# Sparse attention: scores from queries and keys split in two rounded parts, a head's high part and remainder stacked in 128 rows

## The chip, the cores and the metric

The kernel runs on one core of one Trainium2 chip. The metric is the device time of one execution in microseconds (us), as the median of several runs. All names of engines are those of the profile: PE is the matrix engine, PEld its weight loads, DVE the vector engine, ACT the scalar engine, POOL the GpSimd engine, SP the engine that queues the transfers.

## The reference, cut to what matters

The reference computes one block with pooling and sparse attention, and then a second block of two layers. Only the scores of the first block's attention are changed. Of its three branches (compressed, selected, window) the last two have, at 512 positions, scores of every query against every earlier key:

```
q  = partial_rope(rms_norm(q, q_norm_g), positions)      # 8 heads of 64, in 2 groups of 4
ks = partial_rope(rms_norm(k_sel, k_norm_g[1]), positions)   # one key head per group
kw = partial_rope(rms_norm(k_win, k_norm_g[2]), positions)
s = jnp.einsum('bqgrd,bgqkld->bgrqkl', qc, ksel) * scale     # selected blocks
p = masked_softmax(s, m_sel, (-2, -1))
s = jnp.einsum('bqgrd,bkgd->bgrqk', qc, kwc) * scale         # window
p = masked_softmax(s, m_win, -1)
return gc[..., 0:1] * o_cmp + gc[..., 1:2] * o_sel + gc[..., 2:3] * o_win
```

The sequence is 512 long, a head has 64 dimensions.

## The kernel before

**Numbers.** Activations lie transposed, channels on the 128 partitions and the 512 positions along the row. Every large product of weights and activations is made of three products in the rounded type F32R: both operands are split into a high part (rounded copy) and a remainder, and high by high, high by remainder and remainder by high are added in one accumulator bank. ACT makes the high part `wh` of a weight tile (`head`, line 1205) and POOL its remainder `wl` (`rest`, line 519, four instructions of 128x256 each). The scores are different: they are plain F32 products of the queries `qall` and the keys `kk`.

**Order of the first block.** PE works through tiles 0 to 11 of the input projection, then values and gates (`vg_highs`, `vg_lows`, tiles 12 to 14). Meanwhile DVE finishes norm and rotation of six pieces, in `rotated(0)` to `rotated(5)`: the two keys `kk[:, 0]` and `kk[:, 1]` and the four query pairs `qall[:, 0]` to `qall[:, 3]`. One such piece is 128x512: rows 0 to 63 belong to the head of group 0, rows 64 to 127 to that of group 1. Then comes the attention stage, 32 steps `p`, written out by hand: query pair j = p // 8, branch b = p // 4 % 2, query tile i = p % 4. Step p covers 128 queries against n = 128 (i + 1) keys.

**One step on PE** is: `score(p)`; in some steps `cmp_scores`, `values`, `cmp_turn`; `turn_probs(p - 2)`; and then `fill`, products of the pooling branch (lines 627, 628 and 633) that keep PE at work while DVE and ACT deal with the scores. `score(p)` makes one product for each group, the first from rows 0 to 63 and the second from rows 64 to 127, into the banks `SB[0]` and `SB[1]`, and first waits for the exponentials of step p - 1 (`exp_ready`), since there is one bank for each group.

**One step on the others.** DVE takes the masked maximum (`top`, line 1641), and normalizes the probabilities of the step before (`scale`, lines 1964 and 1967); in steps of j = 0 and 1 it also makes tables for the later layers (`steps(tables2, 2)`, lines 1696 to 1722). ACT makes the exponentials (`exps`, line 1361), and copies the turned probabilities (`puts`, line 1205). Every engine works through its list in order. All transfers are queued by SP; POOL issues none and does only `rest` here. The `sqacc` row is cleared by DVE early (line 1852) and used again after the attention.

Of the kernel before, what the change touches and what calls it, by code (L numbers as in the profile page):

```python
# [33 lines left out]
P = 128  # L34
# [124 lines left out]
def build(nc, x, positions, positions2, weights, par1, par2, consts, masks, masks2, w1, w2, pool_w, out):  # L159
    ctx = ExitStack()  # L160
    with ctx:
        base = -(-nc.sbuf_base // (4 * S)) * (4 * S)
        top = [base]

        def at(name, shape, dt, offset):
            return nc.alloc_sbuf_tensor_at(name, list(shape), dt, offset=offset)

        def sb(name, shape, dt=F32):
            size = int(np.prod(shape[1:])) * (2 if dt == BF16 else 4)
            t = at(name, shape, dt, top[0])  # L170
            top[0] += -(-size // 64) * 64
            return t

# [54 lines left out]
        def c2(name, i=0):  # L228
# [67 lines left out]
        hh = big("hh", 0, [P, KF, S], F32R)  # L296
        hl = big("hl", KF, [P, KF, S], F32R)

        cpad = big("cpad", 0, [P, 2, TAPS - 1 + S])
        conv = big("conv", 3, [P, 2, S])  # L300
        ya = big("ya", 5, [P, 2, S])
# [40 lines left out]
        x_landed = [sem(f"x_landed{i}") for i in range(4)]  # L342
        gains_landed = sem("gains_landed")
        par_landed = sem("par_landed")
        late_landed = sem("late_landed")
        cmsk_landed = sem("cmsk_landed")
        shift_landed = sem("shift_landed")
# [27 lines left out]
            "conv_ready", "silu_ready", "prod_ready", "h_hi", "h_lo",  # L375
            "glu_out", "tap_prod", "tap_added", "v_psum", "v_out", "v_rest", "rope_in", "lam_in", "lam_psum", "lam_exp", "lam_ready", "glu_sig", "conv_done", "conv_out",
            "qk_ready", "head_normed", "ya_ready", "ln_sub", "ln_sq", "ln_scaled", "yc_ready", "y_hi", "y_lo",
            "zeroed", "warm", "first_hi", "first_lo", "row_scale", "half_tile", "last_added", "last_sq", "last_sum", "pool_bc", "rstd_out", "pool_out", "out_ready", "par_ready")}
        R = ready
        block = ctx.enter_context(nc.Block())  # L380

# [129 lines left out]
        def _(pool):  # L511
# [24 lines left out]
                x_.then_inc(lo_ready, 1)  # L536

            first_rest()
            with pool.Fori(1, T_BLOCK1) as t:
                rest(Count(0).loop(t, 1))  # L540

            for l in range(LAYERS):
                T = Count(T_BLOCK1).loop(l, T_LAYER)
# [31 lines left out]
        def _(pe):  # L575
# [315 lines left out]
            def score(p):  # L891

                j, b, i = p // 8, p // 4 % 2, p % 4
                n = (i + 1) * P
                if p:
                    pe.wait_ge(R["exp_ready"], 2 * p)
                for g in range(2):
                    h = slice(g * 64, (g + 1) * 64)
                    mm(SB[g][:, 0:n], qall[h, j, i * P:n], kk[h, b, 0:n], start=True, stop=True)\  # L899
                        .then_inc(R["s_psum"], 1)  # L900

            def cmp_scores(j):
# [300 lines left out]
        def _(act):  # L1203
# [98 lines left out]
            def tile_root(m):  # L1302
                root(Count(m - 1), 8, scale=1.0 / 64)

            act.wait_ge(chunk_done, 4)
            head(Count(5))
            tile_square(2, 1)
# [12 lines left out]
            for n in range(6, N_IN):  # L1320
                act.wait_ge(chunk_done, n + 1)
                head(Count(n + 2))
                if n < 9:
                    tile_root(n - 1)
                if n < 8:
                    tile_square(n, n + 1)
                if n in (9, 10):
                    hidden_cmp(n - 9)
                if n == 11:
                    act.wait_ge(R["cmp_copied"], 1)  # L1330
                    act.activation(csq, kcf, ACT.Square).then_inc(sq_ready, 1)
                    act.wait_ge(R["vct_psum"], 1)
                    copy(vct, BC[0:64, 0:P]).then_inc(R["vct_ready"], 1)
                    root(Count(7), 2, parts=32, scale=1.0 / 64)
                if n == 13:
                    act.activation(small[:, 190:191], zero, ACT.Tanh)
                if 10 <= n < 14:
                    pool_head(n - 10)
                if n == 13:
                    act.wait_ge(R["row_scale"], 1)  # L1340
                    vg_out(0, vg_psum, 1, tile_out)
                    vg_out(3, vg_psum, 2, tile_out)
                    vg_out(2, vg_psum, 3, tile_out)
                    vg_out(1, chunk_done, T_IN, tr_read)
# [38 lines left out]
            for p in range(NP):  # L1383
                j, k = p // 8, p % 8
                t, n = T_IN + 3 * j, N_IN + 4 * j
                exps(p)
                if k == 1:
                    act.wait_ge(R["c_sub"], j + 1)
                    act.activation(cmp_p[:, :, :], cmp_p[:, :, :], ACT.Exp).then_inc(R["c_exp"], 1)
                if k == 4:  # L1390
                    act.wait_ge(R["c_tpsum"], j + 1)
                    copy(cmp_pt[:, :], TR[0:64, :]).then_inc(R["c_tready"], 1)
                if p >= 2:
                    puts(p - 2)
                if k == 0 and j:
                    next_head(t - 1)
                if k == 2 and j:
                    out_head(j - 1)
                if k in (3, 6):
                    next_head(t + k // 3 - 1)  # L1400
                if k in (4, 7):
                    gate(n, 0 if k == 4 else 1)
# [230 lines left out]
        def _(dve):  # L1633
# [129 lines left out]
            def rotated(i):  # L1763
                dve.wait_ge(turn1_landed[i % 2], 64 * (i // 2 + 1))
                tt(tmp2[:, 0:S], turned1[:, i % 2, :], sin[:, :], ALU.mult).then_inc(rot_read, 1)
                dve.drain()
                tt(dsts[i], tmp2[:, 0:S], cosp[:, i % 2, :], ALU.add)

            dsts = [kk[:, 0, :], kk[:, 1, :]] + [qall[:, c, :] for c in range(4)]
            gains = [c1("sel_g"), c1("win_g")] + [q_g8] * 4  # L1770
# [78 lines left out]
            dve.drain()  # L1849
            for m in (2, 3, 0, 1):  # L1850
                take(Count(3), Count(m), kvraw[:, m, :] if m < 2 else ybuf[:, m % 2, :], bank_=X4[m])
            dve.memset(sqacc[:, :], 0.0)
            steps(tables1, 2)
            pair_recips(Count(1), 8)
            steps(tables1, 1)
# [119 lines left out]
            for p in range(NP):  # L1975
# [17 lines left out]
                if j < 2 and k not in (0, 2):  # L1993
                    if p == 1:
                        dve.wait_ge(late_landed, 16 * 7)
                    steps(tables2, 2)
            scale(NP - 1)
            pool_gated(NT - 1, 1)
            out_rest(NT - 1)
# [471 lines left out]
```

## Time and profile before

| what | value |
|---|---|
| median of 3 runs | 1873.36 us (1872.85 to 1874.01) |
| the profiled execution | 1872.83 us, span 1871.0 us |
| PE, PEld | 1854.5 us (99%), 1500.5 us (80%) |
| POOL | 1106.2 us (59%) |
| DVE | 856.4 us (46%) |
| ACT | 728.6 us (39%) |
| attention stage, first score to last | 109.1 to 245.3 us |

Busy time of PE is the union of its instructions' times, and its matmuls are pipelined, so 99% doesn't mean that each product runs at its best rate. The time from one instruction's start to the next one's start, which the timeline shows, says what an instruction costs PE.
### The profile page before, as it was taken

To read this page: it belongs to the slowest core of one execution; us is meant where nothing else is said; L and a number is where in the kernel's file an instruction comes from. 1 tells how busy PE (TensorE), PEld (TensorE's weight loads), DVE (VectorE), ACT (ScalarE), POOL (GpSimd) and SP (SyncE) were. 2 spreads that over 40 slices of the span, in tenths; PEclk is the share of its full clock that TensorE was granted. 3 is DMA by queue.
4 is the path that set the end of the run, shared out by engine and by line. 5 is a ranking of instruction groups with operands and counts; after the bars stand their busy time and mean duration, and the time that the engine had idled before them with its cause. 6 is when DMAs were issued, how large, how long until landed. Compare 5 with 4: busy or idle time off the path is not lost.

```text
span 1871.0 us, 28766 instructions
## 1 busy us (share of the span) xinstructions
PE 1854.5 (99%) x8696; PEld 1500.5 (80%) x8696; DVE 856.4 (46%) x1383; ACT 728.6 (39%) x1169; POOL 1106.2 (59%) x1312
## 2 busy tenths in 40 slices
PE   9999999999999999999999999999999999999998
PEld 8866678888888888767888888888867888888887
DVE  7887644465555122876532333112776533333112
ACT  5255543433232223475432323232476433232222
POOL 5532245566667565875656565666775565655654
PEclk9999999999999999999999999999999999999999
DMA  7221123322332333321223322333422223222332
GB/s 268 65 70 46 45 71 99 101 91 91 99 97 93 113 101 102 113 80 57 90 91 100 101 90 101 101 102 102 122 66 71 90 90 101 90 101 92 103 109 79
DMA packets 52407, 177.50 MB, mean 95 GB/s; under 512 B 6832, under 2 KB 8112, under 8 KB 52080
## 3 DMA queue, kind: packets, MB, share of 16 engines
q1 hardware_dynamic: 52336, 176.57, 28.9%
q8 instruction: 43, 0.70, 0.2%
q14 instruction: 28, 0.23, 0.0%
HBM read 168.84 MB, written 2.10 MB: 91 GB/s over the span
## 4 chain that ended last, share of the span: by engine, by line
PE 92%; DVE 4%; ACT 2%; DVEq 1%; issue 1%; DMA 0%; POOL 0%; SPq 0%; POOLq 0%; ACTq 0%
PE bank L613 23%; PE bank L593 23%; PE bank L594 23%; PE bank L650 3%; PE bank L657 3%; PE bank L651 3%; PE bank L899 1%; PE bank L946 1%; PE bank L627 1%; PE bank L628 1%; PE bank L932 1%; PE bank L633 1%; PE bank L734 1%; PE bank L721 1%; PE bank L713 1%; PE bank L714 1%
## 5 line engine op out<-in xcount | busy, mean ns | idle before, releaser
L519 POOL TENSOR_TENSOR wl<-raw,wh (+1 forms) x1240 | 1014.6, 849 | 717.6 <-ACT wh L1205 717.1
L1205 ACT ACTIVATE wh<-raw 128x1024 fp32r (+2 forms) x312 | 329.9, 1058 | 823.1 <-PE bank L613 678.0
L593 PE MATMUL bank<-xh,wh 128*128 128x512 f32 x1312 | 514.0, 392 | 0.0
L594 PE MATMUL bank<-xl,wh 128*128 128x512 f32 x1312 | 510.9, 389 | 0.0
L613 PE MATMUL bank<-xh,wl 128*128 128x512 f32 x1312 | 332.2, 392 | 0.0
L593 PEld LDWEIGHTS bank<-xh,wh 128*128 128x128 f32 x1312 | 246.8, 188 | 52.1 <-ACT lv L1205 0.7
L594 PEld LDWEIGHTS bank<-xl,wh 128*128 128x128 f32 x1312 | 246.4, 188 | 50.5
L613 PEld LDWEIGHTS bank<-xh,wl 128*128 128x128 f32 x1312 | 243.9, 188 | 51.7 <-issue 2.5
L593 PE MATMUL bank<-hh,wh 128*128 128x512 f32 x506 | 196.8, 389 | 0.0
L594 PE MATMUL bank<-hl,wh 128*128 128x512 f32 x506 | 196.8, 389 | 0.0
L1685 DVE TENSOR_TENSOR ybuf<-bank,rstd 128x512 f32<-128x512 f32 x92 | 63.3, 689 | 226.1 <-PE bank L613 223.8
L2022 DVE TENSOR_TENSOR xs<-xs,bank 128x512 f32<-128x512 f32 (+1 forms) x47 | 31.4, 684 | 235.9 <-PE bank L613 188.3
L613 PE MATMUL bank<-hh,wl 128*128 128x512 f32 x506 | 125.9, 389 | 0.0
L613 PEld LDWEIGHTS bank<-hh,wl 128*128 128x128 f32 x506 | 95.0, 188 | 19.7
L594 PEld LDWEIGHTS bank<-hl,wh 128*128 128x128 f32 x506 | 95.0, 188 | 19.7
L593 PEld LDWEIGHTS bank<-hh,wh 128*128 128x128 f32 x506 | 95.0, 188 | 19.7
L2062 DVE TENSOR_TENSOR tmp<-tmp,ybuf 128x512 f32<-128x512 f32 x66 | 71.7, 1086 | 73.3 <-ACT tmp L1460 73.0
L553 POOL TENSOR_TENSOR conv<-conv,tprod 128x512 f32<-128x512 f32 x60 | 83.7, 1395 | 26.0 <-ACT tprod L1205 18.2
L2064 DVE TENSOR_TENSOR hl<-tmp,hh 128x512 f32 (+1 forms) x66 | 60.8, 922 | 58.7 <-ACT hh L1205 58.7
L1685 DVE TENSOR_TENSOR tmp<-bank,rstd 128x512 f32<-128x512 f32 x78 | 53.8, 690 | 59.6 <-PE bank L613 40.6
L1205 ACT ACTIVATE hh<-tmp 128x512 f32 (+1 forms) x66 | 41.8, 633 | 82.0 <-DVE tmp L2062 82.0
L650 PE MATMUL bank<-xh,wh 128*128 128x512 f32 x160 | 62.8, 393 | 0.0
(337 smaller groups left out, 2334.3 us busy)
## 6 DMA issues: line engine op xcount, KB each, us to landing
raw<-in_weights SPq DMA_DIRECT2D x311, 512.0 KB, 3.4
turned<-ybuf SPq DMA_DIRECT2D x64, 64.0 KB, 2.0
xs<-in_x SPq DMA_DIRECT2D x4, 512.0 KB, 6.7
out_t<-outs SPq DMA_DIRECT2D x8, 256.0 KB, 2.3
w1k<-in_w SPq DMA_DIRECT2D x1, 1024.0 KB, 9.5
w1v<-in_w SPq DMA_DIRECT2D x1, 1024.0 KB, 11.0
shifted<-kvraw SPq DMA_DIRECT2D x8, 124.0 KB, 2.3
posi<-in_positions SPq DMA_DIRECT2D x2, 256.0 KB, 8.7
```

Source lines behind the costliest of these rows:

```text
L519: x_ = pool.tensor_tensor(wl[:, :, :].rearrange("p s n -> p (s n)")[:, two], raw[:, cols((v % 4) * (CB * P) + h * part, part)], wh[:, :, : ...
L553: pool.tensor_tensor(conv[:, 1, :], conv[:, 1, :], tprod[:, k % 4, :], ALU.add)\
L593: mm(b[:, :], w, kh(k), start=first and k == 0, stop=False)
L594: mm(b[:, :], w, kl(k), start=False, stop=False)
L613: i = mm(b[:, :], wl[:, s, (blk0 + k) * P:(blk0 + k + 1) * P], kh(k), start=False, stop=last and k == blocks - 1)
L650: mm(X4[a][:, :], w, kh(k), start=k == 0, stop=False)
L651: mm(X4[a][:, :], w, kl(k), start=False, stop=False)
L657: i = mm(X4[a][:, :], wl[:, s, (4 * kk + a) * P:(4 * kk + a + 1) * P], kh(2 * c + kk), start=False, stop=c == 3 and kk == 1)
L1205: return act.activation(o, i, ACT.Copy, scale=scale)
L1685: return tt(o, b[:, :], rstd[:, :], ALU.mult).then_inc(tile_out, 1)
L2062: tt(tmp[:, 1, :], tmp[:, 0, :], ybuf[:, 0, :], ALU.mult).then_inc(R["prod_ready"], 1)
L2064: tt(flat(hl)[:, cols(j * S, S)], tmp[:, 1, :], flat(hh)[:, cols(j * S, S)].bitcast(F32), ALU.subtract).then_inc(R["h_lo"], 1)
```

## The change

Each of the six pieces gets a stacked form and a low part, both in F32R. For query pair or key i, `STACKED[i][g]` is 128x512: for a query, the rows of the group's own half hold its high part and the other 64 rows hold its remainder; for a key, both halves hold the high part. `LOW_PART[i]` is the remainder. A score is then, for each group, one product over 128 rows (high and remainder of the query by the high part of the key) and one over 64 rows (high part of the query by the remainder of the key), added in the same bank.

ACT copies the high parts (`high_part`), POOL subtracts (`low_part`) and moves 64 rows of each to the other half with two transfers from its own queue, six pieces in all. DVE only signals. The clearing of `sqacc` moves to the end of the attention, since its place holds a stacked key.

```diff
+        STACKED = [[row(f"stacked{i}{g}", place) for g, place in enumerate(pair)] for i, pair in enumerate((
+            (45, where["sqacc"]), (39, 43), (46, where["cos"]), (38, 41), (12, 13), (39, 43)))]
+        LOW_PART = [row(f"low_part{i}", place) for i, place in enumerate((8, 42, 9) + 3 * (where["sin"],))]
+        PART_OF = [kk[:, 0, :], qall[:, 0, :], kk[:, 1, :], qall[:, 1, :], qall[:, 2, :], qall[:, 3, :]]
+        KEY_PART, QUERY_PART = (0, 2), (1, 3, 4, 5)
...
             first_rest()
-            with pool.Fori(1, T_BLOCK1) as t:
-                rest(Count(0).loop(t, 1))
+            def low_part(i):
+
+                pool.wait_ge(R["part_hi"], i + 1)
+                if i > 3:
+                    pool.wait_ge(part_landed[i - 1], 32)
+                pool.tensor_tensor(LOW_PART[i], PART_OF[i], STACKED[i][0].bitcast(F32), ALU.subtract)\
+                    .then_inc(R["part_lo"], 1)
+                pool.wait_ge(R["part_lo"], i + 1)
+                for half, dest in enumerate(STACKED[i]):
+                    own, other = slice(half * 64, half * 64 + 64), slice(64 - half * 64, 128 - half * 64)
+                    moved = dest if i in KEY_PART else LOW_PART[i]
+                    pool.dma_start(dest[other, :], moved[own, :]).then_inc(part_landed[i], 16)
+
+            at_ = 1
+            for end, parts in ((12, (0,)), (13, (1,)), (17, (2, 3)), (20, (4,)), (23, (5,)), (T_BLOCK1, ())):
+                with pool.Fori(at_, end) as t:
+                    rest(Count(0).loop(t, 1))
+                for i in parts:
+                    low_part(i)
+                at_ = end
...
                 if p:
                     pe.wait_ge(R["exp_ready"], 2 * p)
+                key, query = KEY_PART[b], QUERY_PART[j]
+                if p in (0, 4):
+                    pe.wait_ge(part_landed[key], 32)
+                if i == 0 and b == 0:
+                    pe.wait_ge(part_landed[query], 32)
+                for g in range(2):
+                    mm(SB[g][:, 0:n], STACKED[query][g][:, i * P:n], STACKED[key][g][:, 0:n], start=True, stop=False)
                 for g in range(2):
                     h = slice(g * 64, (g + 1) * 64)
-                    mm(SB[g][:, 0:n], qall[h, j, i * P:n], kk[h, b, 0:n], start=True, stop=True)\
+                    mm(SB[g][:, 0:n], STACKED[query][g][h, i * P:n], LOW_PART[key][h, 0:n], start=False, stop=True)\
                         .then_inc(R["s_psum"], 1)
...
+            def high_part(i):
+
+                act.wait_ge(R["kq_ready"], (1, 3, 2, 4, 5, 6)[i])
+                a, b = STACKED[i]
+                copy(a, PART_OF[i])
+                copy(b[64:128, :], PART_OF[i][64:128, :]).then_inc(R["part_hi"], 1)
+
...
                 if n in (9, 10):
                     hidden_cmp(n - 9)
+                    high_part(n - 9)
...
                 if p >= 2:
                     puts(p - 2)
+                if p == 1:
+                    act.wait_ge(rot_read, 7)
+                    high_part(2)
+                if p == 2:
+                    high_part(3)
+                if p == 10:
+                    act.wait_ge(R["part_lo"], 4)
+                    high_part(4)
+                if p == 18:
+                    high_part(5)
...
-                tt(dsts[i], tmp2[:, 0:S], cosp[:, i % 2, :], ALU.add)
+                tt(dsts[i], tmp2[:, 0:S], cosp[:, i % 2, :], ALU.add).then_inc(R["kq_ready"], 1)
...
-            dve.memset(sqacc[:, :], 0.0)
             steps(tables1, 2)
...
                     steps(tables2, 2)
+            dve.memset(sqacc[:, :], 0.0)
             scale(NP - 1)
```

The pieces are numbered in the order of `PART_OF`: 0 and 2 are the keys, 1, 3, 4 and 5 the query pairs.

## Rows read from the trace of the kernel before

**Rows 1.** The page: span, and busy time of each engine.
```profile
span 1871.0 us, 28766 instructions
...
PE 1854.5 (99%) x8696; PEld 1500.5 (80%) x8696; DVE 856.4 (46%) x1383; ACT 728.6 (39%) x1169; POOL 1106.2 (59%) x1312
```

**Rows 2.** Busy time by stretch: length, PE, PEld, DVE, ACT, POOL, granted clock, DMA.
```profile
178.00:214.00 36.00, 36.00 (x201) 23.84 (x200) 23.45 (x81) 19.96 (x58) 8.46 (x13) 1.00 0.13 45
```

**Rows 3.** Timeline of PE, the three scores that it waits for.
```profile
124.00 0.49 PE L899 MATMUL bank<-kk,qall 64*128 64x128 f32 x4 [0.18 <-ACT probs L1361]
...
131.72 0.92 PE L899 MATMUL bank<-kk,qall 64*128 64x384 f32 x4 [0.64 <-ACT probs L1361]
...
163.91 0.70 PE L899 MATMUL bank<-kk,qall 64*128 64x256 f32 x4 [0.41 <-ACT probs L1361]
```

**Rows 4.** Timeline of PE, 180 to 211 us.
```profile
180.34 0.40 PE L628 MATMUL bank<-xl,wh 128*128 128x512 f32 x1
...
183.07 0.39 PE L628 MATMUL bank<-xl,wh 128*128 128x512 f32 x1
183.38 0.70 PE L899 MATMUL bank<-kk,qall 64*128 64x256 f32 x4
184.02 1.09 PE L932 MATMUL bank<-cst,probs 128*128 128x128 f32 x8
...
196.19 0.49 PE L899 MATMUL bank<-kk,qall 64*128 64x128 f32 x4
196.61 0.88 PE L932 MATMUL bank<-cst,probs 128*128 128x128 f32 x6
197.25 0.48 PE L627 MATMUL bank<-xh,wh 128*128 128x512 f32 x1
...
205.90 1.12 PE L951 MATMUL bank<-cmp_pt,small 64*128 64x512 f32 x2
...
209.15 1.13 PE L899 MATMUL bank<-kk,qall 64*128 64x512 f32 x4
210.21 0.66 PE L932 MATMUL bank<-cst,probs 128*128 128x128 f32 x4
```

**Rows 5.** Timeline of PE in the last tile, F32R products of 256 columns.
```profile
1849.04 2.08 PE L1048 MATMUL bank<-hh,wl 128*128 128x256 f32 x16
1850.96 0.28 PE L1042 MATMUL bank<-hh,wh 128*128 128x256 f32 x1
```

**Rows 6.** Timeline of ACT, 115 to 123 us.
```profile
115.95 0.42 ACT L1389 ACTIVATE cmp_p<-cmp_p 128x256 f32<-128x256 f32 x1 [0.56 <-DVE cmp_p L1928]
118.51 0.58 ACT L1361 ACTIVATE probs<-bank,small 128x384 f32<-128x384 f32 x1 [2.14 <-DVE small L1641]
...
122.49 0.69 ACT L1361 ACTIVATE probs<-bank,small 128x512 f32<-128x512 f32 x1 [2.41 <-DVE small L1641]
```

**Rows 7.** Timeline of POOL around the stage's first steps.
```profile
111.74 2.80 POOL L519 TENSOR_TENSOR wl<-raw,wh  x4 [2.38 <-ACT wh L1205]
125.80 3.83 POOL L519 TENSOR_TENSOR wl<-raw,wh  x4 [11.26 <-ACT wh L1205]
```

**Rows 8.** The page: costliest groups, and transfers.
```profile
L553 POOL TENSOR_TENSOR conv<-conv,tprod 128x512 f32<-128x512 f32 x60 | 83.7, 1395 | 26.0 <-ACT tprod L1205 18.2
...
L1205 ACT ACTIVATE hh<-tmp 128x512 f32 (+1 forms) x66 | 41.8, 633 | 82.0 <-DVE tmp L2062 82.0
...
shifted<-kvraw SPq DMA_DIRECT2D x8, 124.0 KB, 2.3
```

**Rows 9.** Timeline of DVE, beside POOL at work until 213.1 us and behind it.
```profile
212.41 0.95 DVE L1967 TENSOR_SCALAR probs<-probs,small,small 128x512 f32<-128x512 f32 x1
...
213.51 0.55 DVE L1967 TENSOR_SCALAR probs<-probs,small,small 128x512 f32<-128x512 f32 x1
```

**Rows 10.** Timelines of DVE and of PE at the start.
```profile
35.11 0.48 DVE L1852 MEMSET sqacc<- 128x512 f32 x1
...
37.95 0.66 PE L742 MATMUL bank<-cst,pairs 128*128 128x128 f32 x4 [0.32 <-DVE pairs L1669]
```

More of the change, by code:

```diff
@@ L163, in build @@
         top = [base]
+        where = {}
         def at(name, shape, dt, offset):
@@ L170, in sb @@
             t = at(name, shape, dt, top[0])
+            where[name] = top[0]
             top[0] += -(-size // 64) * 64
@@ L297, in build, with row @@
         hl = big("hl", KF, [P, KF, S], F32R)
+        PART_OF = [kk[:, 0, :], qall[:, 0, :], kk[:, 1, :], qall[:, 1, :], qall[:, 2, :], qall[:, 3, :]]
+        def row(name, place):
+            return at(name, [P, S], F32R, place if place > 100 else BIG + place * UNIT)[:, :]
+        STACKED = [[row(f"stacked{i}{g}", place) for g, place in enumerate(pair)] for i, pair in enumerate((
+            (45, where["sqacc"]), (39, 43), (46, where["cos"]), (38, 41), (12, 13), (39, 43)))]
+        LOW_PART = [row(f"low_part{i}", place) for i, place in enumerate((8, 42, 9) + 3 * (where["sin"],))]
+        KEY_PART, QUERY_PART = (0, 2), (1, 3, 4, 5)
         cpad = big("cpad", 0, [P, 2, TAPS - 1 + S])
@@ L344, in build @@
         par_landed = sem("par_landed")
+        part_landed = [sem(f"part_landed{i}") for i in range(6)]
         late_landed = sem("late_landed")
@@ L377, in build @@
             "qk_ready", "head_normed", "ya_ready", "ln_sub", "ln_sq", "ln_scaled", "yc_ready", "y_hi", "y_lo",
-            "zeroed", "warm", "first_hi", "first_lo", "row_scale", "half_tile", "last_added", "last_sq", "last_sum", "pool_bc", "rstd_out", "pool_out", "out_ready", "par_ready")}
+            "zeroed", "kq_ready", "part_hi", "part_lo", "warm", "first_hi", "first_lo", "row_scale", "half_tile", "last_added", "last_sq", "last_sum", "pool_bc", "rstd_out", "pool_out", "out_ready", "par_ready")}
         R = ready
```

## The prediction

> **What bounds the kernel now.** I read the page first: PE is busy 1854.5 of 1871.0 us [rows 1], so time is gained only where PE is kept shorter, or made to wait less. Then the busy times by stretch: from 178 to 214 us, in the middle of the attention stage, PE is busy 36.00 of 36 us, while no other engine reaches 24 [rows 2]. There a microsecond less on PE is a microsecond less in the end. Before that it is not so: PE waits for exponentials in steps 4, 6 and 13, together 1.23 us [rows 3], because DVE makes tables there beside its share of the scores. Last, the timeline of PE, start to start, gives what the score products cost.
>
> **What the scores cost now.** From the start of a score to the start of what follows it, 128, 256 and 512 columns take 0.42, 0.64 and 1.06 us [rows 4]. This is 0.207 us plus 1.667 ns a column; that slope is four passes at 2.4 GHz (0.417 ns a column each). 384 columns are then 0.85. A score comes 0.31 us after a product that costs 0.2275 (twelve of them in 2.73 us, 180.34 to 183.07), so entering it costs 0.085 more [rows 4]. The two groups run side by side: one 64-row product of 512 columns alone (line 951) lasts 1.12 us, and the two of a score 1.13 [rows 4]. So the four lengths, entry included, are 0.505, 0.725, 0.932 and 1.145 us, 3.31 in all, eight times over.
>
> **What they cost after.** F32R makes one pass instead of four, but there are two products now, and the 128-row ones of the two groups fill the array and go one after the other.
> - Two 128-row products: 2 x 0.2275 at 512 columns [rows 4], 2 x 0.120 at 256 (sixteen in 1.92 us) [rows 5], the middle, 2 x 0.174, at 384. No row has F32R at 128 columns. The nearest are the transposes of 128 columns, six in 0.64 us, 0.107 each [rows 4]; twice the 256 is the other end in time per column, four passes a third (0.213). I take 0.107: the array is no emptier than there, and the weights are of the same size.
> - Entering the 64-row products: 0.085, as now. The 128-row ones follow the fill products in the same form, so they pay no entry.
> - The 64-row pair, side by side: one pass, 0.053, 0.107, 0.160, 0.213. That F32R pairs also overlap is in no row; if not, it costs a full product more (0.107 to 0.2275), 0.63 for four lengths.
> - The constant 0.207: an F32 product is two records, an F32R one only one. I take it as 0.104 for each round of records, so half of it goes. The ends are none of it gone and all of it gone, 3.3 us up or down in 32 steps.
>
> Sums: 0.46, 0.54, 0.70 and 0.86, together 2.55 instead of 3.31. Eight times 0.76 is **6.1 us less on PE**.
>
> **What of it is lost.** Savings of steps 2 to 6 (0.24 + 0.29 + 0.05 + 0.19 + 0.24 = 1.0) come before waits that DVE and ACT set [rows 3]; PE just waits longer. For step 13 I count 0.2 more. 1.2 us are lost; nothing to 2 are the bounds.
>
> **Piece by piece.** Each piece is two copies on ACT, 0.63 us each by the nearest form [rows 8], some 1.2 us. Pieces 0 and 1 are made while the projection runs; they are wanted only at 109 us. Piece 2 comes at step 1, behind the exponential that starts at 115.95 and lasts 0.42, so it ends at 117.6; the next exponential isn't due before 118.51, for ACT waits 2.14 us there. Piece 3 comes at step 2, behind two small copies, at 120.0, and ends at 121.3, before 122.49 [rows 6]. Pieces 4 and 5 stand in the same sort of gap; behind piece 4 stands `out_head(0)`, which is wanted a step later. ACT costs nothing; without these gaps it would be up to 1.2 us a piece.
>
> POOL subtracts: 1.4 us a piece [rows 8]. Beside it DVE slows: the same operation takes 0.95 us with POOL at work and 0.55 without [rows 9]. This counts only where DVE sets the time, pieces 2 and 3; one operation on the path each, 2 x 0.4 = **0.8 us more** (0 to 1.6). The work itself fits: POOL is free from 114.5 to 125.8 [rows 7]. The wait for `part_hi` holds back `rest(12)`, `rest(13)`, `rest(17)`, `rest(20)` and `rest(23)`, and so the remainders that PE wants and the weight loads behind them on SP; each has some microseconds until it is due, since PE first does the tile's high products.
>
> Twelve transfers of 128 KB are issued by POOL. No row has a transfer from POOL; SP's 124 KB one lands 2.3 us after its issue [rows 8]. Piece 2 is the only tight one: subtracted at 117.6 + 1.4 = 119.0, landed at 121.3 by that row, wanted by step 4 at 124.00 [rows 3]. That leaves 2.7 us for what POOL needs to issue two transfers. I cost it at nothing; once the cover is gone, each microsecond later is one at the end. The Trainium skill, page "SBUF — State Buffer", section "SBUF: two separate sides", has a rule against this: GpSimd writes its own descriptors, and while VectorE runs an operation that takes the shared port it can't. No row shows it, for POOL issues nothing before the change. By it the landing moves by the operations met, 0.55 us each [rows 9]: four of them are 2.2 us and still inside the 2.7, so the sum stays, and of the late landing's chance below half is owed to it.
>
> The cleared `sqacc` leaves the start: 0.48 us of DVE [rows 10] ahead of a PE wait of 0.32 us; **0.3 us less** (nothing to 0.3). At its new place DVE waits for the last exponential anyway.
>
> **The sum.** -6.1 + 1.2 + 0.8 - 0.3 = **-4.4 us**. The profiled execution took 1872.83 us (span 1871.0 and 1.83 around it), 0.5 below the median of 1873.36. From that median: **1869.0 us**, 0.23% less. What a measurement of this kernel can tell from no change is about 0.2%, 3.75 us; the forecast is just past it.
>
> **Rivals.**
> - *Narrow products cost more.* If F32R at 128 columns makes four passes, the two 128-row products cost 2 x 0.106 more and the pair 0.160: 0.37 in eight steps, 3.0 us. For it: no row under 256 columns. Against: 0.120 at 256 shows no step upwards. 1872.0 us.
> - *The constant stays.* The entry and exit of a 64-row group, not the records, make up the 0.207: 3.3 us more, 1872.3.
> - *The 64-row pair doesn't overlap in F32R.* 8 x 0.63 = 5.0 more: 1874.0. Against: F32 does overlap in the same rows and banks.
> - *Slower: piece 2 lands late.* POOL takes long to issue, and step 4 stands still. Place: the wait for `part_landed[2]`. It eats the gain of 4.4 when it lands at 128.4 + the 2.7 of cover counted, that is 7.1 us behind my estimate of 121.3, and is slower by over 0.2% from 10.9 behind on; at 13 us the end is 1879. For it: nothing bounds POOL's issue from above. Against: SP's transfer of the same size took 2.3 us in all [rows 8], a fifth of what it needs.
> - *Larger gain.* All of the constant goes: 1865.7.
>
> **How the numbers follow.** Forecast 0.58, on its own between 1867 and 1870.5, two thirds of it past the bound; narrow products 0.12; constant stays 0.12; no overlap 0.07; late landing 0.06 (0.04 of it slower), larger gain 0.05. The predicted time is 1869.0. Down to 1866.3 and up to 1873.8 leaves out half of the larger gain, the late landing and most of no overlap, under 0.2. Faster by over 0.2%: 0.58 x 0.66 + 0.05 = 0.43. Slower: 0.05. The same: 0.52.
>
> **What the profile after would show.** Score groups of 0.46, 0.54, 0.70 and 0.86 us, start of the first 128-row product to the next instruction; the 64-row pair with starts a few nanoseconds apart; waits for ACT before steps 4, 6 and 13 grown to some 2.4 us; no wait of PE for a transfer; the wait at 37.95 gone. I am wrong if the 128-column products take over 0.15 us each, if the 64-row products come one after the other, or if PE stands still for `part_landed`.

## The result, and the profile after

The changed kernel takes 1876.54 us (median of 22 runs, 1874.19 to 1877.89); the kernel before takes 1873.24 beside it (22 runs, 1872.35 to 1874.10). The ratio is 1.0018, with a 95% interval of 1.0013 to 1.0024: 3.3 us slower, where 4.4 us less was forecast. The result lies outside the range, and its sign is the other one. One of the eleven runs of "piece 1 later" below took 3226.41 us at a mean granted clock of 0.647, and its ratio leaves that run out.

The profiled execution took 1876.28 us. Its page answers to [rows 1] as follows; the last line is the new queue of POOL.

```profile
span 1874.4 us, 28801 instructions
...
PE 1854.7 (99%) x8696; PEld 1510.0 (81%) x8696; DVE 860.3 (46%) x1383; ACT 735.4 (39%) x1181; POOL 1120.6 (60%) x1330
...
q0 software_dynamic: 960, 1.57, 0.4%
```

The span is 3.4 us longer and PE is busy for as long as before, so on the page alone nothing seems to have become faster. The waits of PE over the first 262 us say more (total, times, longest):

```profile
PE bank L869 <- DVE ybuf L1741: 3.4, 1, 3.4
PE bank L934 <- ACT probs L1407: 3.3, 4, 1.4
```

The first is new. The second answers to [rows 3], which had 1.23 us in three. The timeline of PE shows where they lie, and where the attention stage begins and ends:

```profile
37.23 0.60 PE L773 MATMUL bank<-cst,pairs 128*128 128x128 f32 x4
...
98.20 0.40 PE L869 MATMUL bank<-wh,xh 128*128 128x280 f32 x1 [3.36 <-DVE ybuf L1741]
...
103.42 0.29 PE L869 MATMUL bank<-wh,xh 128*128 128x280 f32 x1
...
113.47 0.33 PE L934 MATMUL bank<-stacked,stacked 128*128 128x128 f32 x2
...
125.26 0.73 PE L934 MATMUL bank<-stacked,stacked 128*128 128x512 f32 x2 [1.35 <-ACT probs L1407]
...
130.48 0.44 PE L934 MATMUL bank<-stacked,stacked 128*128 128x128 f32 x2 [1.19 <-ACT probs L1407]
...
144.43 0.61 PE L934 MATMUL bank<-stacked,stacked 128*128 128x512 f32 x2
...
248.41 0.63 PE L934 MATMUL bank<-stacked,stacked 128*128 128x512 f32 x2
```

In the kernel before, the scores of steps 0, 7 and 31 (the last two have 512 columns) start at 109.13, 138.28 and 244.22 us. These three starts cut the execution into four stretches, and each stretch answers one question:

| stretch | before | after | difference |
|---|---|---|---|
| start to step 0: projection, with pieces 0 and 1 | 109.13 | 113.47 | +4.34 |
| step 0 to 7: DVE and ACT set the time, pieces 2 and 3 | 29.15 | 30.96 | +1.81 |
| step 7 to 31: PE sets the time | 105.94 | 103.98 | -1.96 |
| step 31 to the end of the span | 1626.8 | 1626.0 | -0.8 |

**The gain is there, in the third stretch, but small.** Three lengths of score groups in that stretch, start of the first 128-row product, start of the 64-row pair, start of what follows:

```profile
148.18 0.33 PE L934 MATMUL bank<-stacked,stacked 128*128 128x128 f32 x2
148.45 0.33 PE L937 MATMUL bank<-low_part,stacked 64*128 64x128 f32 x2
148.71 0.28 PE L948 MATMUL bank<-cmsk 128*128 128x256 bf16 x1
...
153.54 0.40 PE L934 MATMUL bank<-stacked,stacked 128*128 128x256 f32 x2
153.87 0.39 PE L937 MATMUL bank<-low_part,stacked 64*128 64x256 f32 x2
154.18 1.09 PE L970 MATMUL bank<-cst,probs 128*128 128x128 f32 x8
...
162.21 0.63 PE L934 MATMUL bank<-stacked,stacked 128*128 128x512 f32 x2
162.77 0.50 PE L937 MATMUL bank<-low_part,stacked 64*128 64x512 f32 x2
163.20 0.66 PE L970 MATMUL bank<-cst,probs 128*128 128x128 f32 x4
```

The groups take 0.53, 0.64 and 0.99 us, and the one of 384 columns 0.81 (156.96 to 157.77): 2.97 for the four lengths, where 2.55 was forecast and 3.31 were needed before. At 512 columns the two 128-row products take 0.56, of which 2 x 0.2275 = 0.455 is the products; the pair takes 0.43, of which 0.213 is one pass over 512 columns. So about 0.1 is lost on the way into the pair and 0.2 on the way out.

**The first loss: one small DVE operation.** DVE in the first stretch, and then POOL (there, and beside steps 1 and 2 of the attention):

```profile
91.85 1.63 DVE L1839 TENSOR_TENSOR tmp<-tmp 128x512 f32<-128x512 f32 x1
...
94.17 2.94 DVE L1845 TENSOR_TENSOR small<-tmp,cst 128x16 f32<-128x16 f32 x1
...
97.45 0.69 DVE L1741 TENSOR_TENSOR ybuf<-bank,rstd 128x512 f32<-128x512 f32 x1
```

```profile
91.19 1.74 POOL L557 TENSOR_TENSOR low_part<-qall,stacked 128x512 fp32r<-128x512 f32 x1
93.23 1.06 POOL L563 DMA_DIRECT2D stacked<-low_part  x2 [0.29 <-POOL low_part L557]
94.30 2.77 POOL L532 TENSOR_TENSOR wl<-raw,wh  x4
...
121.97 1.29 POOL L557 TENSOR_TENSOR low_part<-kk,stacked 128x512 fp32r<-128x512 f32 x1 [2.98 <-ACT stacked L1243]
123.56 1.06 POOL L563 DMA_DIRECT2D stacked<-stacked  x2 [0.30 <-POOL low_part L557]
126.79 1.28 POOL L557 TENSOR_TENSOR low_part<-qall,stacked 128x512 fp32r<-128x512 f32 x1 [2.17 <-ACT stacked L1243]
```

The 128x16 operation of line 1845 takes 0.17 us elsewhere (at 85.67). Here it takes 2.94 and ends at 97.11, when the four back-to-back instructions of `rest(13)` end on POOL (94.30 + 2.77 = 97.07). Behind it on DVE stands the operation that empties PE's bank (97.45), and PE waits 3.36 us for that. In the kernel before DVE was 0.99 us ahead of POOL here; DVE's operation and `rest(13)`:

```profile
93.81 0.17 DVE L1789 TENSOR_TENSOR small<-tmp,cst 128x16 f32<-128x16 f32 x1
```

```profile
94.80 3.96 POOL L519 TENSOR_TENSOR wl<-raw,wh  x4 [2.23 <-ACT wh L1205]
```

Now DVE is 0.4 us later, held at 91.85 beside the subtraction of piece 1 (1.63 us), and `rest(13)` is 0.5 us earlier, so that they start 0.13 us apart, DVE first.

**The pause costs more than its length.** Busy times by stretch just behind it (length, PE, PEld, DVE, ACT, POOL, granted clock, DMA):

```profile
98.80:100.00 1.20, 1.20 (x5) 0.81 (x4) 1.05 (x3) 0.00 (x0) 0.00 (x0) 0.51 0.88 348
100.00:102.00 2.00, 2.00 (x7) 0.87 (x6) 1.74 (x5) 0.23 (x1) 0.00 (x0) 0.50 0.04 12
102.00:103.00 1.00, 1.00 (x8) 1.00 (x8) 0.52 (x1) 0.98 (x2) 0.00 (x0) 0.88 0.00 0
```

The granted clock is 0.50, the level of 1.2 GHz, from 98.8 to some 102.2 us; in the kernel before it is 1.00 in this stretch. From the product that waited (98.20) to the first product of the next tile (103.42) PE takes 5.22 us; the same instructions took 3.56 before (95.41 to 98.97). These are 1.66 us more. So the first stretch is 3.36 + 1.66 - 0.7 (from the earlier start at 37.23) = 4.3 longer.

**The second loss: steps 2 and 3.** The two halves of DVE's `scale`, one not beside a subtraction and one beside it, in step 2 and in step 3:

```profile
121.32 0.41 DVE L2022 TENSOR_SCALAR probs<-probs,small,small 128x256 f32<-128x256 f32 x1
...
121.88 1.53 DVE L2022 TENSOR_SCALAR probs<-probs,small,small 128x256 f32<-128x256 f32 x1
...
126.15 0.48 DVE L2022 TENSOR_SCALAR probs<-probs,small,small 128x384 f32<-128x384 f32 x1
...
126.78 1.50 DVE L2022 TENSOR_SCALAR probs<-probs,small,small 128x384 f32<-128x384 f32 x1
```

They take 1.1 and 1.0 us longer and end 0.15 and 0.2 us behind the end of POOL's subtraction (121.97 + 1.29 = 123.26, and 128.07). [Rows 9] had shown 0.4 for such a meeting.

**What held.** ACT's copies lie in the gaps: the exponential behind the first pair of copies waits 2.08 us for DVE, not for ACT.

```profile
120.63 1.26 ACT L1243 ACTIVATE stacked<-kk 128x512 fp32r<-128x512 f32 x2
123.98 0.58 ACT L1407 ACTIVATE probs<-bank,small 128x384 f32<-128x384 f32 x1 [2.08 <-DVE small L1697]
```

POOL issues two transfers in 1.06 us (1.22 for the pair of piece 0), and they land 2.4 us after issue (last number):

```profile
stacked<-low_part POOLq DMA_DIRECT2D x8, 128.0 KB, 2.4
...
stacked<-stacked POOLq DMA_DIRECT2D x4, 128.0 KB, 2.4
```

Piece 2 is thus there about 127.0 us (issue from 123.56, 1.06, 2.4), and step 4 wants it at 130.48. PE has no wait for a transfer.

**The last stretch differs, though its code is the same.** In the second block PE has pauses that differ between the profiled executions. From 745 to 860 us, before and then after:

```profile
745.00:860.00 115.00, 112.89 (x549) 85.03 (x548) 90.99 (x151) 76.02 (x153) 89.07 (x91) 1.00 0.29 89
```

```profile
745.00:860.00 115.00, 114.56 (x556) 87.40 (x555) 87.48 (x147) 73.55 (x149) 91.69 (x95) 1.00 0.30 92
```

PE is idle 2.1 us in the one and 0.4 in the other, but the changed kernel does the same work 4.2 us later, and a pause of 0.5 us that lies inside the window before lies behind it after. Over the whole last stretch PE is idle 11.5 us before and 10.8 after, which is the difference of 0.8. Between 1624.9 and 1627.7 us lie the last stretches of all the kernels below. A single span therefore doesn't settle a difference of less than some 3 us; the first three stretches are compared for that, beside the medians.

### The profile page after: what moved, and what is told of

It reads as the page before. It is cut to its first block, busy times and chain, and to the rows that moved or that the text cites. A ratio compares the mean times of both kernels' runs of the same rounds, so it can differ in the third digit from the quotient of the medians.

```text
span 1874.4 us, 28801 instructions
## 1 busy us (share of the span) xinstructions
PE 1854.7 (99%) x8696; PEld 1510.0 (81%) x8696; DVE 860.3 (46%) x1383; ACT 735.4 (39%) x1181; POOL 1120.6 (60%) x1330
## 4 chain that ended last, share of the span: by engine, by line
PE 91%; DVE 5%; ACT 2%; DVEq 1%; issue 1%; DMA 0%; SPq 0%; POOL 0%; POOLq 0%; ACTq 0%
PE bank L644 23%; PE bank L624 23%; PE bank L625 23%; PE bank L681 3%; PE bank L688 3%; PE bank L682 3%; PE bank L984 1%; PE bank L970 1%; DVE bank L1693 1%; PE bank L664 1%; PE bank L658 1%; PE bank L659 1%; PE bank L765 1%; PE bank L1160 1%; ACT lp L1587 1%
```

## The experiments

My theory after the result had three parts: **(A)** the products save 2.8 us in 32 steps, not 6.1, because the constant of 0.2 us stays whole, beside a way in of about 0.1; **(B)** the pause at 98.20 comes from the meeting of DVE with `rest(13)` that piece 1 brings about; **(C)** the subtractions of pieces 2 and 3 hold DVE in steps 2 and 3. The rivals: the products gave what was forecast and the rest is all contention, or the new waits are owed to something else (the transfers, the moved clearing, ACT's copies). Each ran against the kernel before on the same chip.

| kernel | ratio (95%) | median, before beside it | to step 0 | 0 to 7 | 7 to 31 | rest |
|---|---|---|---|---|---|---|
| before | | | 109.1 | 29.15 | 105.94 | 1626.8 |
| after | 1.0018 (1.0013 to 1.0024) | 1876.54, 1873.24 | 113.5 | 30.96 | 103.98 | 1626.0 |
| products alone | 0.9989 (0.9980 to 0.9998) | 1871.27, 1873.36 | 108.9 | 29.09 | 104.00 | 1627.5 |
| all but the products | 1.0030 (1.0018 to 1.0041) | 1878.39, 1873.36 | 112.2 | 31.03 | 105.94 | 1625.5 |
| piece 1 later | 1.0000 (0.9991 to 1.0010) | 1873.50, 1873.36 | 108.8 | 31.22 | 104.02 | 1627.1 |
| narrow subtraction | 0.9977 (0.9968 to 0.9986) | 1868.90, 1873.36 | 109.0 | 28.86 | 103.95 | 1625.1 |
| clearing alone | 0.9999 (0.9990 to 1.0008) | 1873.14, 1873.33 | 108.5 | 29.16 | 105.96 | 1627.7 |
| tables later | 0.9993 (0.9984 to 1.0002) | 1871.89, 1873.33 | 109.4 | 27.46 | 106.20 | 1627.6 |
| piece 1 and tables later | 0.9986 (0.9977 to 0.9995) | 1870.51, 1873.33 | 108.7 | 28.32 | 104.23 | 1627.6 |
| the same, DVE subtracts 2 and 3 | 0.9984 (0.9975 to 0.9993) | 1870.30, 1873.33 | 108.8 | 27.87 | 104.27 | 1627.6 |
| after, whole rows | 1.0002 (0.9993 to 1.0011) | 1873.62, 1873.33 | 114.6 | 30.88 | 101.26 | 1624.9 |
| DVE subtracts, whole rows | 0.9969 (0.9957 to 0.9981) | 1867.44, 1873.33 | 109.1 | 27.28 | 102.19 | 1626.6 |
| the same, group after group | 0.9966 (0.9954 to 0.9978) | 1866.80, 1873.33 | 108.7 | 27.12 | 101.48 | 1627.3 |

The four columns on the right are of the profiled executions, from the starts of the scores of steps 0, 7 and 31.

**The products alone.** The kernel before, with queries and keys written in F32R and the score as one 128-row and one 64-row product on them; no split, no copy, no transfer. The scores are those of rounded operands, and each has a product over 128 rows that mixes both groups.

```diff
+                    mm(SB[g][:, 0:n], qr[:, j, i * P:n], kr[:, b, 0:n], start=True, stop=False)
+                for g in range(2):
                     h = slice(g * 64, (g + 1) * 64)
-                    mm(SB[g][:, 0:n], qall[h, j, i * P:n], kk[h, b, 0:n], start=True, stop=True)\
+                    mm(SB[g][:, 0:n], qr[h, j, i * P:n], kr[h, b, 0:n], start=False, stop=True)\
```

> The kernel before with the new products alone: for each group a 128-row and a 64-row F32R product on the unstacked queries and keys. It leaves out splitting and stacking, so the sums in the banks are others; ACT, POOL and the transfers are as before. Theory A (the products gain about half of what was forecast, and POOL's work costs more than that): groups of 0.53, 0.64, 0.81 and 0.99 us instead of 0.505, 0.725, 0.93 and 1.145, 2.8 us less on PE, 0.7 of it swallowed by waits of the first steps: 2.1 us less, 0.9989 of before. Theory B (the products gain nothing in the end): 1.000. The forecast as made: 4.9 us less, 0.9974.

1871.27 us, 2.1 us less, ratio 0.9989. Steps 7 to 31 take 104.00 us, as in the changed kernel. (A) holds: the products give about 2 us, and 6.1 was never to be had from them.

**All but the products.** The changed kernel, with its pieces, copies and transfers, but with scores as F32 products of 64 rows on the high parts alone.

```diff
-                for g in range(2):
-                    mm(SB[g][:, 0:n], STACKED[query][g][:, i * P:n], STACKED[key][g][:, 0:n], start=True, stop=False)
...
-                    mm(SB[g][:, 0:n], STACKED[query][g][h, i * P:n], LOW_PART[key][h, 0:n], start=False, stop=True)\
+                    mm(SB[g][:, 0:n], STACKED[query][g][h, i * P:n].bitcast(F32), STACKED[key][g][h, 0:n].bitcast(F32), start=True, stop=True)\
```

> The changed kernel with plain F32 64-row products as before, on the stacked high parts; the remainders are made and moved, but left out of the scores. It holds all the overheads and none of the products' gain. Theory A: 2 us slower than the changed kernel, ratio to before 1.0028. Theory B (products worth nothing, overheads small): as the changed kernel, 1.0018.

1878.39 us, 5 us more than before: this is what making the pieces costs. Steps 7 to 31 are back at 105.94, to the hundredth; the pause of 3.4 us is there, and steps 0 to 7 are as long as in the changed kernel. Its profiled execution (1876.60 us) is the fastest of its seven, and its clock did not fall behind the pause (below). The two halves of the change add up: -2.1 and +5.0 make +2.9, and +3.3 was measured.

**Piece 1 later.** POOL subtracts piece 1 behind `rest(13)` instead of ahead of it.

```diff
-            for end, parts in ((12, (0,)), (13, (1,)), (17, (2, 3)), (20, (4,)), (23, (5,)), (T_BLOCK1, ())):
+            for end, parts in ((12, (0,)), (14, (1,)), (17, (2, 3)), (20, (4,)), (23, (5,)), (T_BLOCK1, ())):
```

> The changed kernel with piece 1 made by POOL behind the remainder of tile 13 instead of ahead of it. Theory A (POOL, late by piece 1, starts tile 13's four subtractions just as a short DVE operation is to begin, holds it for 2.8 us, and PE waits 3.4 us for the tile DVE takes next): the wait of 3.4 us goes, 2.5 to 3.4 us faster than the changed kernel, 1.0000 to 1.0005 of before. Theory C (the wait comes from ACT's copies or the transfers of piece 1): no change, 1.0018.

1873.50 us, 3.0 less than the changed kernel. The pause is gone, the granted clock is 1.00 from 94 to 104 us, and step 0 starts at 108.81 instead of 113.47. The operation that was held takes its usual time; the second line is the one that empties the bank:

```profile
93.47 0.17 DVE L1845 TENSOR_TENSOR small<-tmp,cst 128x16 f32<-128x16 f32 x1
...
93.98 0.69 DVE L1741 TENSOR_TENSOR ybuf<-bank,rstd 128x512 f32<-128x512 f32 x1
```

(B) is shown, as far as the order on POOL is its cause. Nothing was done to the length of `rest(13)` itself, and the hold also starts while POOL still issues the second transfer (until 94.29), which this edit moves as well; the next run bears on that.

**A narrow subtraction.** POOL subtracts 16 of 512 columns; the high part stands in the place of the remainder in the transfers and the products. The remainders are left out of the scores.

```diff
-                pool.tensor_tensor(LOW_PART[i], PART_OF[i], STACKED[i][0].bitcast(F32), ALU.subtract)\
+                pool.tensor_tensor(LOW_PART[i][:, 0:16], PART_OF[i][:, 0:16], STACKED[i][0][:, 0:16].bitcast(F32), ALU.subtract)\
...
-                    moved = dest if i in KEY_PART else LOW_PART[i]
+                    moved = dest
...
-                    mm(SB[g][:, 0:n], STACKED[query][g][h, i * P:n], LOW_PART[key][h, 0:n], start=False, stop=True)\
+                    mm(SB[g][:, 0:n], STACKED[query][g][h, i * P:n], STACKED[key][g][h, 0:n], start=False, stop=True)\
```

> The changed kernel with POOL's subtraction cut from 512 to 16 columns; the low part is left out of the scores (a high part stands in its place), copies, waits, transfers and products are all there. Theory A (the length of the subtraction holds DVE off its operations): the two DVE operations of 1.5 us in steps 2 and 3 are 0.4 to 0.5 again, and the wait of 3.4 us at 98 us goes or shrinks: 2 to 5.5 us faster than the changed kernel, 0.9989 to 1.0007 of before. Theory C (transfers or ACT's copies cost it): as the changed kernel, 1.0018.

1868.90 us. Both losses are gone: no pause at 98 us, though piece 1 and its transfers still stand ahead of `rest(13)` (DVE's small operation starts at 93.80, `rest(13)` at 94.75), and steps 0 to 7 take 28.86 us instead of 31.22 with piece 1 later. The operation beside POOL's subtraction in step 2, and that subtraction:

```profile
117.39 0.45 DVE L2022 TENSOR_SCALAR probs<-probs,small,small 128x256 f32<-128x256 f32 x1
```

```profile
117.46 0.22 POOL L557 TENSOR_TENSOR low_part<-kk,stacked 128x16 fp32r<-128x16 f32 x1 [2.98 <-ACT stacked L1243]
```

(C) is shown: 2.4 us in steps 0 to 7 hang on the length of the subtractions, and not on the copies or the transfers, which are all still there. The kernel was some 2 us faster than I had expected. In the profiled execution that lies in the last stretch, 1625.1 us against 1627.1, where its instructions are those of the others. The median shows the same 2 us, so it belongs to this kernel and not to one execution; its cause is open.

**The clearing alone.** The kernel before, with the clearing of `sqacc` moved.

```diff
-            dve.memset(sqacc[:, :], 0.0)
             steps(tables1, 2)
...
+            dve.memset(sqacc[:, :], 0.0)
             scale(NP - 1)
```

> The kernel before with the clearing of sqacc moved to the end of the attention, as in the change, and nothing else. As forecast: the PE wait of 0.3 to 0.6 us at 38 us goes, 0.9998. If it is worth 2 us, which the difference of the two earlier runs (new products alone, narrow subtraction) would allow, 0.9989.

1873.14 beside 1873.33 us, and the interval includes no change. In the profile the wait of 0.32 us [rows 10] is gone, and step 0 starts 0.6 earlier. It is no cause of a loss.

**Tables later.** The kernel before, with DVE's tables out of steps 0 to 7 and one instruction at a time in the steps behind.

```diff
-                if j < 2 and k not in (0, 2):
-                    if p == 1:
-                        dve.wait_ge(late_landed, 16 * 7)
-                    steps(tables2, 2)
+                if p == 1:
+                    dve.wait_ge(late_landed, 16 * 7)
+                if j and k not in (0, 2):
+                    steps(tables2, 1)
```

> The kernel before with DVE's table steps for the later layers taken out of the steps of query pair 0 and spread over those of pairs 1 to 3, one a step. Theory D (DVE's tables make PE wait in steps 4, 6 and 13): those waits of 1.2 us go, 0.9993. If another engine sets them: 1.000.

1871.89 us, 1.4 less; steps 0 to 7 take 27.46 instead of 29.15. So the waits of [rows 3] were DVE's own load, worth 1.4 us already in the kernel before.

**Both, in the changed kernel.** Piece 1 later and tables later.

> The changed kernel with piece 1 behind tile 13 and with the tables moved as in the run before. Theory A with D: DVE has 8 us less to do in pair 0, so POOL's two subtractions of 1.1 us each on its way are covered, and PE's waits of 3.6 us for exponentials shrink below 1.5 us: 2 to 3 us faster than with piece 1 alone moved, 0.9985 to 0.999 of before. If the waits come from the chain score, maximum, exponential itself: 1.000, as without the tables.

1870.51 us: 6.0 less than the changed kernel, 2.8 less than the kernel before. **The same, with pieces 2 and 3 subtracted by DVE** instead of POOL; in its profile each subtraction takes DVE 0.69 us.

```diff
+                if p in (2, 3):
+                    dve.wait_ge(R["part_lo"], p)
+                    dve.wait_ge(R["part_hi"], p + 1)
+                    tt(LOW_PART[p], PART_OF[p], STACKED[p][0].bitcast(F32), ALU.subtract).then_inc(R["part_lo"], 1)
```

> As the run before, but pieces 2 and 3 are subtracted by DVE itself behind its maxima of steps 2 and 3 (0.7 to 1.0 us each) and POOL only moves them. Theory A: no operation of DVE is held for over a microsecond in these steps, PE's waits go below 1 us: as the run before or up to 1 us faster, 0.998 to 0.9988 of before. A rival: piece 2 then lands some 2 us later than with POOL, and PE waits for it in step 4 by up to 1 us: 0.999.

1870.30 us. Steps 0 to 7 are 0.45 us shorter; in the medians the two can't be told apart.

**What is the constant?** A step of the prediction was still open: 0.207 us of each score, beside the 0.1 on the way in, that no count of columns explains. Either it is the way into and out of 64-row products, or it comes with each round of products on a bank. This tells them apart: the second product over all 128 rows, the stacked query by the whole row of the key's remainders. The added rows multiply the remainder of one group's query by the remainder of the other group's key, a term of second order.

```diff
-                    h = slice(g * 64, (g + 1) * 64)
-                    mm(SB[g][:, 0:n], STACKED[query][g][h, i * P:n], LOW_PART[key][h, 0:n], start=False, stop=True)\
+                    mm(SB[g][:, 0:n], STACKED[query][g][:, i * P:n], LOW_PART[key][:, 0:n], start=False, stop=True)\
```

> The changed kernel, with the second product of each group over all 128 rows instead of 64: stacked query by the whole row of key remainders. The rows that are added multiply a remainder of one group's query by a remainder of the other group's key. Theory (the 0.2 us constant of a score, and the 0.1 before it, are the way into and out of a 64-row product): no product of a score has 64 rows any more, both are gone, and a score is four products of 0.107, 0.120, 0.174 or 0.2275 us: groups of 0.43, 0.48, 0.70 and 0.91 us instead of 0.53, 0.64, 0.81 and 0.99, which is 0.45 x 8 = 3.6 us less, some 3 of it outside waits; ratio to before 1.0002 instead of 1.0018. Rival (the constant comes with each round of a score, whatever its rows): two more full products stand in place of a side-by-side pair, 0.16 + 0.13 + 0.19 + 0.24 = 0.72 a quartet, 5.8 us more; ratio 1.005.

1873.62 us, 2.9 less than the changed kernel, although PE now streams twice as many columns for the second product. Two groups of its timeline:

```profile
149.13 0.33 PE L934 MATMUL bank<-stacked,stacked 128*128 128x128 f32 x2
149.30 0.39 PE L936 MATMUL bank<-low_part,stacked 128*128 128x128 f32 x2
149.53 0.28 PE L947 MATMUL bank<-cmsk 128*128 128x256 bf16 x1
...
162.79 0.63 PE L934 MATMUL bank<-stacked,stacked 128*128 128x512 f32 x2
163.25 0.62 PE L936 MATMUL bank<-low_part,stacked 128*128 128x512 f32 x2
163.71 0.60 PE L969 MATMUL bank<-cst,probs 128*128 128x128 f32 x4
```

The groups take 0.40 and 0.92 us instead of 0.53 and 0.99, which is four products and hardly a constant; that of 256 columns takes 0.47 instead of 0.64. The one of 384 takes 0.79 instead of 0.81: behind it come products with a tile of 64 columns (128*64), and my reading is that the array's shape still changes there. No run was made for it, but in step 2 of this trace, where a 128*128 product follows (at 122.34), the group of 384 takes 0.71 us. Steps 7 to 31 take 101.26 us. The rival, 5.8 us more, is out. The Trainium skill, page "TensorEngine Tiling (Array Packing)", section "Key Properties", says that changing the tiling mode drains the engine; the trace agrees, and puts 0.1 us on the way in and 0.2 on the way out.

This run still has the pause at 98 us. Its clock there, and that of the run with everything but the products:

```profile
98.00:103.00 5.00, 4.58 (x15) 3.06 (x16) 4.19 (x12) 0.50 (x2) 0.00 (x0) 0.50 0.35 107
```

```profile
98.00:103.00 5.00, 4.63 (x31) 3.86 (x32) 4.38 (x14) 2.28 (x4) 0.00 (x0) 1.00 0.32 107
```

The first ran at half the clock throughout, the second at the full one, after the same pause. The pause thus costs 3.4 us plus something that is 0.1 us in one execution (98.37 to 102.05 for what took 3.56 before), 1.66 in another and 2.5 in a third (98.42 to 104.51). The 22 runs of the changed kernel spread over 3.7 us and those of before over 1.75, which fits.

**Whole rows in the best version so far** (piece 1 and tables later, DVE subtracts 2 and 3):

> The version with piece 1 behind tile 13, the tables spread over the later steps and pieces 2 and 3 subtracted by DVE (ratio 0.9984), with the second product of each group over all 128 rows. Theory: 3 us less than that version, ratio 0.9968. Rival (constant stays): 5.8 us more, ratio 1.0015.

1867.44 us, 2.9 less again.

**And the products of group 0 ahead of those of group 1:**

```diff
                 for g in range(2):
                     mm(SB[g][:, 0:n], STACKED[query][g][:, i * P:n], STACKED[key][g][:, 0:n], start=True, stop=False)
-                for g in range(2):
                     mm(SB[g][:, 0:n], STACKED[query][g][:, i * P:n], LOW_PART[key][:, 0:n], start=False, stop=True)\
                         .then_inc(R["s_psum"], 1)
```

> As the run before it, and the two products of group 0 ahead of the two of group 1, so that group 0's maximum can begin before group 1's products. Group 0's bank is complete 0.1 to 0.45 us earlier, group 1's at the same time. Theory: it counts only where PE waits for the exponentials, three or four steps: 0 to 0.5 us less than the run before it, ratio 0.9966. Rival (two products into one bank one behind the other cost more than two into different banks): 0.05 us or more for each of 32 steps, 1.6 us more, ratio 0.9977.

1866.80 us, the fastest: 6.4 to 6.5 less than the kernel before. Steps 7 to 31 are 0.7 us shorter than in the run before it. Two products into one bank one behind the other cost nothing extra: the groups keep their lengths, and the difference is shorter waits for ACT (0.4 instead of 1.1 us from 134 to 240).

## Why the prediction was wrong, step by step

- **"The constant 0.207 ... half of it goes": wrong, and 3.3 of the 6.1 us with it.** I took the constant for the count of records and named its other reading as a rival. It is the change of shape, and it stays whole: 2.97 us for four lengths where 3.31 were needed before and 2.55 forecast, so 0.34 x 8 = 2.7 us less instead of 6.1. The rival "the constant stays" was right on this term, with its 3.3 us. [Rows 4] had a hint that I read but did not use: behind a 128-row product a 64-row one started 0.085 us late, so a change of shape had a price on the way in, and might have had one on the way out.
- **"Pieces 0 and 1 ... are wanted only at 109 us": true, and the wrong question.** What mattered was what POOL's new work does to DVE at that time, 91 to 97 us. I had costed contention only "where DVE sets the time, pieces 2 and 3". DVE empties the banks of the projection as well, so it can set the time there too: 3.36 us of pause and 1.66 of lower clock. This is the largest term, and I had it at nothing. The work itself moved little: `rest(13)` merely came to stand a tenth of a microsecond behind a short operation of DVE that the bank was waiting for.
- **"2 x 0.4 = 0.8 us" for pieces 2 and 3: the mechanism was right, the size off.** The two operations took 1.1 and 1.0 us longer, 2.1 in all, and steps 0 to 7 were 2.4 us shorter in the run with the narrow subtraction. The 0.4 of [rows 9] was a meeting with the tail of POOL's instruction; a whole meeting lasts as long as the subtraction, 1.29 us. Both figures lie past my upper bound of 1.6.
- **What is lost in the first steps: right in kind.** With the products alone steps 0 to 7 take 29.09 us instead of 29.15, though their groups should be 0.6 us shorter by the rows above (0, 0.085, 0.125, 0.155 a length). But the waits before scores grow only from 1.23 to 1.45 us, in steps 3, 4, 6 and 13; the rest goes into groups behind a wait, which are 0.1 us longer, and into gaps behind the groups. In the changed kernel these waits are 3.3 us, where "some 2.4 us" was forecast: that the number comes near is chance, for most of it is the hold by the subtractions and not the swallowed gain.
- **The covers: right.** ACT costs nothing, and pieces 4 and 5 neither (105.94 us for steps 7 to 31 with everything but the products, as before); piece 2 has 3.5 us to spare, with POOL's issue taking 1.06 us for two transfers; no wait for `part_landed`. The sentence that the prediction takes from the Trainium skill, page "SBUF — State Buffer", section "SBUF: two separate sides", that VectorE can keep GpSimd from writing its descriptors, is not borne out here. The pairs of pieces 2 and 3 had no DVE operation of the kind that was held beside them, but where DVE subtracts, POOL issues the pair of piece 3 in 1.02 us from 123.97 on, beside such an operation, and neither is slower for it:

```profile
124.18 0.55 DVE L2023 TENSOR_SCALAR probs<-probs,small,small 128x512 f32<-128x512 f32 x1
```

- **The clearing: right**, 0.3 us in the wait, not to be told apart in the median.
- **F32R at 128 columns and the overlap of the 64-row pair: right.** Two products of 128 columns take 0.17 us where nothing changes shape (149.13 to 149.30), and the pair takes 0.26, 0.31 and 0.43 us at 128, 256 and 512 columns with its exit: 0.44 ns a column, which is one pass for both groups and not two.

Put together with the measured sizes: -0.6 for the products of steps 0 to 6 and -2.0 for the others, +2.4 for the longer waits and gaps in steps 0 to 6 (what is left of that stretch's +1.81), +3.4 and +1.7 for the pause and its clock, -0.7 at the start: +4.2. The last score does start 4.2 us later, and the last stretch, which differs by up to 2.8 us between executions of like code, gave 0.8 back.

## What to carry to other kernels

Price a product by its shape and by its neighbours' shape: in F32R a product of 64 rows between products of 128 costs 0.3 us more than its columns, and up to 512 columns a full-height product with harmless extra rows was cheaper. New work on POOL is to be laid beside DVE's timeline in every stage where DVE releases something, not only where DVE is the busiest, and each meeting counts with POOL's whole run of instructions. Where PE waits, look at the granted clock behind the wait before the sum is closed: here it stayed at 1.00 behind waits of 1.2 and 1.35 us, and fell in two of three executions with one of 3.4.

## What the hardware did that I had not expected

- A DVE operation of 128x16 with two operands was held for 2.8 us, over four instructions of POOL in a row, and not only over the one that it met (94.17 to 97.11). The Trainium skill, page "SBUF — State Buffer", section "SBUF: two separate sides", says that the pair of ports is an exclusive lock for a whole instruction, and that whoever starts first has it. In steps 2 and 3 the trace agrees with the lock (1.53 against 0.41 us), but not with the order as recorded: DVE's record starts 0.09 us before POOL's in step 2 (121.88 and 121.97), and DVE is the one held. At 94 us the hold goes beyond one instruction; that it is this lock is my reading.
- The granted clock fell to 1.2 GHz with a pause of 3.4 us, in two of the three executions whose profile has that pause: in the changed kernel 0.6 us behind the pause, for some 3.4 us, and with whole rows within it (at 97.0), for 6.8. In both PE had been busy for 59.44 of the 60 us from 30 to 90 us. The Trainium skill, page "TensorE: Matmul & The Clock Gate", section "Part 1: The HAM clock gate", has such a gate between 1.2 and 2.4 GHz; why one execution escaped it is open.
- The second half of the program, with unchanged code, took 1624.9 to 1627.7 us in thirteen profiled executions. In the four shortest of these stretches DVE is busy for 669.9 to 672.1 us, in the other nine for 672.9 to 675.7, with the same operations. Whether DVE is held by POOL less often in the short ones, no run tests.
